# A gMLP layer on one core: the opening transfers regrouped, the first step's twelve products put ahead of the turns, and GpSimd's adding transfers issued in two groups

## The reference

```python
def rms_norm(x, g):
    return x * lax.rsqrt(jnp.mean(x * x, axis=-1, keepdims=True) + EPS) * g

hn = rms_norm(x, norm1_g)
u, v = jnp.split(jax.nn.gelu(hn @ w_in), 2, axis=-1)
v = (v - mu) * lax.rsqrt(var + LN_EPS) * ln_g            # over v's last axis
v = v.reshape(b, l // 128, 128, 8, 256)
ws = jnp.where(causal, w_s, 0)
sv = jnp.einsum('gts,bnsge->bntge', ws, v) + b_s.T[None, None, :, :, None]
x = x + (u * sv.reshape(b, l, 2048)) @ w_out
x = x + jnp.square(jax.nn.relu(rms_norm(x, norm2_g) @ w1)) @ w2
out = rms_norm(x, final_g)
```

## Time and profile before

| | |
|---|---|
| median of 3 runs | 1066.47 us (1065.72 to 1066.68) |
| profiled execution | 1067.01 us |
| span of its instructions | 1064.9 us |
| mean granted TensorE clock | 0.998 |
| PE busy | 1056.5 us (99%) |
| PEld busy | 928.1 us (87%) |
| DVE, ACT, POOL busy | 798.8 us (75%), 561.4 us (53%), 44.5 us (4%) |
| DMA | 206.40 MB, mean 194 GB/s |

### The profile page before, as it was taken

How to read it: one execution, slowest core, us unless ns; L and a number is a source line. 1 busy time by engine, 2 the same in 40 slices (tenths; PEclk the granted TensorE clock), 3 DMA queues, 4 the chain that set the end, 5 groups by cost and what they waited for, 6 DMA issues and landing times.

```text
span 1064.9 us, 13170 instructions
## 1 busy us (share of the span) xinstructions
PE 1056.5 (99%) x5040; PEld 928.1 (87%) x5040; DVE 798.8 (75%) x892; ACT 561.4 (53%) x883; POOL 44.5 (4%) x49
## 2 busy tenths in 40 slices
PE   9999999999999999999999999999999999999997
PEld 8888888889899888888888888888888888888886
DVE  6986666779789996899858457565599585777766
ACT  6864454553554444564874555455643443344456
POOL 0000100000000000111000000000000000000240
PEclk9999999999999999999999999999999999999999
DMA  9273369772876495755444636627878355343224
GB/s 323 73 166 151 112 208 307 180 262 98 320 281 229 156 338 201 200 190 160 151 166 158 198 118 213 208 106 278 323 296 317 135 218 198 119 158 119 82 77 159
DMA packets 89935, 206.40 MB, mean 194 GB/s; under 512 B 9560, under 2 KB 16240, under 8 KB 82672
## 3 DMA queue, kind: packets, MB, share of 16 engines
q1 hardware_dynamic: 86192, 195.32, 52.6%
q0 software_dynamic: 3488, 9.96, 3.9%
q10 hardware_dynamic: 192, 0.27, 0.1%
HBM read 143.67 MB, written 67.11 MB: 198 GB/s over the span
## 4 chain that ended last, share of the span: by engine, by line
PE 98%; DMA 1%; ACT 0%; DVE 0%; SPq 0%; issue 0%; ACTq 0%; DVEq 0%
PE banks L479 32%; PE banks L483 32%; PE banks L484 32%; PE banks L573 3%; DMA rows<-in_x_dram 1%; PE banks L618 0%; ACT rows L1195 0%; PE banks L604 0%; PE banks L529 0%; PE banks L534 0%; DVE rows L1706 0%; ACT spare L1228 0%; ACT rows L1477 0%; DVE ring_low L1536 0%; ACT ring_high L1047 0%
## 5 line engine op out<-in xcount | busy, mean ns | idle before, releaser
L1077 ACT ACTIVATE pair_high<-left_and_right 128x1024 fp32r<-128x1024 f32 x168 | 176.5, 1055 | 223.3 <-PE banks L479 183.9
L1536 DVE TENSOR_TENSOR ring_low<-left_and_right,ring_high 128x512 fp32r<-128x512 f32 x224 | 152.3, 690 | 160.9 <-ACT ring_high L1047 160.3
L1544 DVE TENSOR_TENSOR pair_low<-left_and_right,pair_high 128x1024 fp32r<-128x1024 f32 x168 | 205.1, 1235 | 84.2 <-ACT pair_high L1077 83.9
L479 PE MATMUL banks<-pair_high 128*128 128x512 f32 x672 | 254.9, 379 | 0.0
L483 PE MATMUL banks<-pair_low,pair_high 128*128 128x512 f32 x672 | 254.7, 379 | 0.0
L484 PE MATMUL banks<-pair_high,pair_low 128*128 128x512 f32 x672 | 254.7, 379 | 0.0
L1047 ACT ACTIVATE ring_high<-left_and_right 128x512 fp32r<-128x512 f32 x224 | 136.9, 626 | 206.6 <-PE banks L479 126.0
L479 PE MATMUL banks<-s_high,ring_high 128*128 128x512 f32 x384 | 145.8, 380 | 0.0
L483 PE MATMUL banks<-s_low,ring_high 128*128 128x512 f32 x384 | 145.5, 379 | 0.0
L484 PE MATMUL banks<-s_high,ring_low 128*128 128x512 f32 x384 | 145.5, 379 | 0.0
L484 PEld LDWEIGHTS banks<-pair_high,pair_low 128*128 128x128 f32 x672 | 127.0, 189 | 18.0
(11 more groups left out here) (147 smaller groups left out, 1244.6 us busy)
## 6 DMA issues: line engine op xcount, KB each, us to landing
left_and_right<-sums SPq DMA_DIRECT2D x40, 1024.0 KB, 7.5
sums<-rows SPq DMA_DIRECT2D x34, 1024.0 KB, 5.2
left_and_right<-in_mlp_w_dram SPq DMA_DIRECT2D x34, 1024.0 KB, 7.3
left_and_right<-in_a_w_in_dram SPq DMA_DIRECT2D x19, 1024.0 KB, 7.6
v_blocks<-rows SPq DMA_DIRECT2D x8, 1024.0 KB, 7.2
left_and_right<-in_a_w_out_dram SPq DMA_DIRECT2D x8, 1024.0 KB, 10.5
rows<-in_x_dram SPq DMA_DIRECT2D x7, 1024.0 KB, 8.8
right_sums<-in_mlp_w_dram POOLq DMA_DIRECT2D x6, 1024.0 KB, 11.2
```

Source lines behind the costliest of these rows:

```text
L479: first = nc.tensor.matmul(ps[:, bank, :], stat_high, mov_high, start=start, stop=False, skip_group_check=True)
L1077: nc.scalar.activation(pair_high[pair_entry(d, pos, k)][:, :, :], pair_of(d, pos, k), ACT.Copy)\
L1536: nc.vector.tensor_tensor(ring_low[k][:, :], right_place(n, pos)[:, k, :], ring_high[k][:, :].bitcast(F32), ALU.subtract).then_inc(low_don ...
L1544: nc.vector.tensor_tensor(pair_low[e][:, :, :], pair_of(d, pos, k), pair_high[e][:, :, :].bitcast(F32), ALU.subtract).then_inc(low_done, 1)
```

## The change

The x of a11's k-tiles 1, 2 and 3 comes in one transfer of 768 KB in the third place of SP's queue. b11's k-tiles 1 and 2 follow it singly, each with a semaphore, ahead of a12; its k-tile 3 comes behind a12. b21 is loaded in two halves of 512 KB with a22 between them. `first_unit` issues its twelve products one after another, and `first_turn(1)` follows them, directly ahead of the turns of k-tiles 2 and 3. The fillers behind the gains' turn are one in place of two. On GpSimd the copies and additions of t1 and t3 wait for b22 of single 1 in place of b22 of single 2, and stand ahead of the causal mask; t2 and t4 stay behind it and wait for b22 of single 2.

```diff
@@ first_unit @@
                     if m == 0:
                         mm.then_inc(unit_begun, 1)
-                first_turn(1)
                 pe.wait_ge(combo_low, 1)
 ...
                     nc.tensor.matmul(ps[:, banks[m], :], rows_high[:, c], walked(ring_low[0][:, :]), start=False,
                                      stop=False, skip_group_check=True)
+                first_turn(1)
@@ first_turn @@
-                pe.wait_ge(x_landed[["a11_first", "a11_second", "a11_right", "a11_right"][k]], 16)
+                pe.wait_ge(x_landed["a11_rest" if k else "a11_first"], 16)
@@ tensor block @@
             first_turn(0)
             turn_gains()
-            warm(2)
+            warm(1)
@@ sync block @@
+            def load_k(b, first, end, signal):
+                i = places(0)[b]
+                sp.dma_start(quarter[i][:, first:end, :], weight(0, b)[:, first:end, :]).then_inc(signal, 16)
+
             load_x("a11_first", 0, 0, P)
-            sp.dma_start(quarter[0][:, 0:1, :], weight(0, "b11")[:, 0:1, :]).then_inc(first_landed, 16)
-            load_x("a11_second", 0, P, P)
-            sp.dma_start(quarter[0][:, 1:2, :], weight(0, "b11")[:, 1:2, :]).then_inc(second_landed, 16)
-            load_x("a11_right", 0, 2 * P, 2 * P)
+            load_k("b11", 0, 1, first_landed)
+            load_x("a11_rest", 0, P, 3 * P)
+            load_k("b11", 1, 2, second_landed)
+            load_k("b11", 2, 3, third_landed)
             load_x("a12", 0, NB, NB)
-            load(("b11", 0), quarter[0][:, 2:4, :], weight(0, "b11")[:, 2:4, :], quarter_landed[0], "quarter0")
+            load(("b11", 0), quarter[0][:, 3:4, :], weight(0, "b11")[:, 3:4, :], quarter_landed[0], "quarter0")
             load_x("a21", 4, 0, NB)
-            load_weight(0, "b21")
+            load(("b21", 0), quarter[1][:, 0:2, :], weight(0, "b21")[:, 0:2, :], quarter_landed[1], "quarter1")
             load_x("a22", 4, NB, NB)
+            load_k("b21", 2, 4, b21_rest_landed)
             load_weight(0, "b12")
@@ split_high, on ACT @@
                 elif u == 1:
                     act.wait_ge(second_landed, 16)
+                elif u == 2:
+                    act.wait_ge(third_landed, 16)
+                elif (n, pos) == (0, 1) and k >= 2:
+                    act.wait_ge(b21_rest_landed, 16)
                 else:
                     right_ready(n, pos)
@@ gpsimd block @@
-            pool.wait_ge(ws_turned, 2)
-            nc.gpsimd.affine_select(out=ws_t[:, :, :], in_=ws_t[:, :, :], compare_op=ALU.is_ge, fill=0.0, base=0,
-                                    pattern=[[0, GROUPS], [1, P]], channel_multiplier=-1).then_inc(ws_masked, 1)
-            pool.wait_ge(*landed["b22", 2])
+            pool.wait_ge(*landed["b22", 1])
             nc.gpsimd.dma_start(t_of("t1"), weight(4, "b11")).then_inc(t_made["t1"], 16)
 ...
             nc.gpsimd.dma_start(t_of("t3"), weight(4, "b22"), accum_op=ALU.add).then_inc(t_made["t3"], 16)
+            pool.wait_ge(ws_turned, 2)
+            nc.gpsimd.affine_select(out=ws_t[:, :, :], in_=ws_t[:, :, :], compare_op=ALU.is_ge, fill=0.0, base=0,
+                                    pattern=[[0, GROUPS], [1, P]], channel_multiplier=-1).then_inc(ws_masked, 1)
+            pool.wait_ge(*landed["b22", 2])
             pool.wait_ge(t_made["t1"], 32)
```

More of the change, by code:

```diff
@@ L296, in summed_of @@
             return (2, 4, 6)[d] + h
-        x_landed = {b: sem(f"x_landed_{b}") for b in ("a11_first", "a11_second", "a11_right", "a12", "a21", "a22")}
+        x_landed = {b: sem(f"x_landed_{b}") for b in ("a11_first", "a11_rest", "a12", "a21", "a22")}
         quarter_landed = [sem(f"quarter_landed{i}") for i in range(4)]
@@ L348, in trunk @@
         second_landed = sem("second_landed")
+        third_landed = sem("third_landed")
+        b21_rest_landed = sem("b21_rest_landed")
         x_summed = sem("x_summed")
```

## The result

The changed kernel takes **1067.88 us** (median of 20 runs, 1067.33 to 1068.68). The kernel before takes 1066.41 us in 20 runs beside them (1065.26 to 1066.87). The ratio is 1.0014, with a 95% interval of 1.0008 to 1.0020: about 1.5 us slower, where 1066.3 was forecast. That is less than 0.2%, and just inside the range, but more than the runs leave uncertain. The profiled execution took 1067.86 us (span 1065.5).

A forecast was written before the change was run, and what follows sets the result against it. TensorE, 98% of the chain, bounds the kernel, so only its waits count. Start +1.0 and stall -1.0 sum to 0.0 against the median 1066.47; leaning 0.2 lower gives 1066.3 us, range 1065.3 to 1067.9.

The forecast's parts named there:

- the adding transfers: GpSimd's additions move earlier, so the load of v takes about 4.7 us and TensorE's wait at 227 goes: -1.0 us.
- the stall: TensorE's wait for DVE's `ring_low` at 226.61 to 227.81 us, sized 1.0 us, expected to go entirely.
- The start: First 16 us: unit 2 starts at 16.0 against 15.02, a cost of 1.0 us, between 0.8 and 1.7.
- Late landing: Rival, chance 0.12: the 768 KB land at 9.5 or later; start +1.7, stall -1.0: 1067.2 us.
- The stall stays: Rival, chance 0.11: load of v slow for other traffic, or t4 past 209; start +1.0, stall 0: 1067.5 us.
- The 0.2 us by which the forecast leaned lower: Taken off the sum because the start's terms have slack: the clock may rise earlier, 0.1 us may not be paid.
- One filler less: Ahead of the first products: a filler takes about 0.43 us, so L521 may start at 5.55 instead of 5.99.
- The twelve products: Start: with eight products moved ahead of the turn of k-tile 1, TensorE is free for it at 8.6.
- The 768 KB: Start: the one transfer of x lands at 8.7, bounds 7.3 to 9.5; the turn of k-tile 1 starts at 8.75.
- What is late next: ACT's and DVE's chain behind the turn: 2.76 us, TensorE idle some 1.5, unit 1 at 11.6, unit 2 4.4 later.
- The clock did not fall back: Rival, chance 0.04: the 1.5 us gap before unit 1 drops TensorE to 1.2 GHz, losing 2.6 us: 1068.9 us.
- Nothing new: Added traffic from 86 to 110 us, or b21's later half, might make TensorE wait; the former got no chance of its own.

The follow-up runs named there:

- e1: The kernel before with only the change's GpSimd part (copies and additions of t1 and t3 earlier): 1066.50 us, ratio 1.0001.
- e3: e1 with the turn of k-tile 1 behind the twelve products and one filler, queue of before: 1068.11 us, ratio 1.0013.
- e6: The kernel before with one more wait ahead of GpSimd's chain of copies and additions, which then began at 156.05 against 155.78: 1066.72 us, ratio 1.0004.
- e5: The changed kernel with the 768 KB cut into two transfers again, 256 KB and 512 KB: 1067.22 us, ratio 1.0011.
- e9_after: One more profiled execution of the changed kernel, unedited: 1067.87 us.
- e7: The changed kernel with the second filler put back: 1067.80 us, ratio 1.0017.
- e2: The changed kernel without its GpSimd part: 1068.61 us, ratio 1.0018.
- e4: The changed kernel with the turn of k-tile 1 back between the four and the eight other products, and two fillers: 1067.72 us, ratio 1.0018.
- e9_before_1: One more profiled execution of the kernel before, unedited: 1066.55 us.
- e8: e1 with b11's k-tile 2 in a transfer of its own, with its own semaphore, ahead of a12: 1066.76 us, ratio 1.0002.

## Why the prediction was wrong

**The step that failed** is "All of it goes: -1.0 us" in *the adding transfers*, which the sum then set against the median. In the change the stall is not there, with the times that were reckoned: additions from 87.67, t4's issued at 184.13, a load of v of 4.8 us, `normalise` 1.77 us sooner though the start was later. But the stall belonged to the one execution that was profiled. In three more of before it is missing. There t4's addition is issued at 201.57 to 201.86 rather than 206.08, and lands, 9.4 to 9.6 us later, at 211.0 to 211.4; the load of v is issued at 209.00 to 209.74 and takes 4.9 to 5.3 us. Seen in one execution of four, the term is worth about 0.25 us and not 1.0, an estimate from few executions, and e1 put it at +0.1 us, between -0.9 and +1.0, which just shuts out the -1.0. The warning stood in the prediction: the profiled execution was 0.5 us above the median of the runs. I read that as an offset to subtract at the end; the trace has the same 0.5 us behind the stall (227.81 against a mean of 227.28 in the other three), so the -1.0 was taken from a time that did not hold it.

**The start** was forecast at +1.0 at unit 2, between 0.8 and 1.7, and this term was too small as well. Unit 2 starts at 15.02 in the mean of the four executions of before and at 16.77 in both of the change: +1.75. The step that missed here is the landing of the 768 KB, 9.5 in place of 8.7, which is the whole difference. Further on the difference shrinks by 0.4 us, since in two of the executions of before the turn of a22 stands for x (1.02 us, and about 0.25), and in the change it does not: the product ahead of the stall's place (226.61, 227.24, 226.61 and 227.34; mean 226.95) comes at 228.32 in both executions of the change, +1.37 us. Less the 0.25 this is +1.1, and the program's last product shows the same (1058.8 against a mean of 1057.7). The profiled times of the six executions give 1067.87 - 1066.54 = +1.3; the medians give +1.47 with an interval of 0.9 to 2.1. So two rivals held in part. "Late landing" describes the start, and against the one profiled execution of before also the sum (+0.7; measured 1067.86 - 1067.01 = +0.85). "The stall stays" has the right worth for the additions at the median, though not the cause: nothing stayed, there was mostly nothing to remove. The 0.2 us by which the forecast leaned lower did not come either.

*One filler less* was priced at 0.43 us; the start of L523 at 5.55 was wrong for the two executions of the change. Its weights were split by ACT at 5.29 + 0.63 = 5.92 in place of 5.48, and TensorE waited for them. ACT itself waited for their landing, and that varies: the split begins at 4.49 to 4.85 in the executions of before, but at 5.29 and 5.05 in e3 and e6, which have the same queue. In e5, where it began at 4.62, L523 did start at 5.57. In e9_after it started at 5.76, and most of the first four products ran at the lower level (1.72 us). e7, with the filler back, has the same median, so it costs and gives nothing that can be measured.

*The twelve products* left TensorE free at 8.66, as reckoned (8.6). *The 768 KB* were taken as 8.7, by bytes between two rows; they landed at 9.5 in both executions of the change, the bound of "late landing", and at 8.6 to 9.3 with the same transfer in e2, e4 and e7 (7.0, 7.4 and 6.8 us after an issue near 1.8). The estimate from the page "DMA: Bandwidth & Descriptors" of the Trainium skill (Anatomy of one DMA), by its 2.0 us and 436 GB/s, was 5.6; no run here had it before 8.6.

*What is late next* held in each term: 2.77 us from the turn to the split's end, a gap of 1.38 us (forecast 1.5), 4.33 us from unit 1 to unit 2 (forecast 4.4). Only the 0.2 us that b11's k-tile 2 was to win is, like the stall, not in every execution of before: from unit 1 to unit 2 it is 4.61 us in the first, 4.67 in e6, and 4.34 to 4.38 in the three others.

*The new order* loses even with x in time. e7 against e6 shows it: +1.86 us at unit 1 and, since e6 then stands at the turn of a22 for x and at 227, +0.4 behind the stall. e5, where x landed near 7.0 while TensorE was busy until 9.99, still has 1.0011. e3's runs show it as well, at 1.0013 (1.4 us) without the large transfer. And e4's show that the large transfer loses without the order, at 1.0018. The two do not add up (e2, with both, has 1.0018, and the change 1.0014), since each alone delays the same chain behind the turn of k-tile 1.

**The clock did not fall back** in the gap: unit 1's products stand 0.22 us apart at once. **Nothing new** waits between 86 and 110 us or in units 4 to 8.

What stays open is the exact share of executions with the stall, which four do not give (with e2 and e6, whose additions begin as in before, it is two of six). Open too is why the chain of additions ran late in the first execution: t4's was issued 4.2 to 4.5 us later than in the other three, and most of that arose behind the issue of t2's addition (187.34, against 186.42 to 187.00). And nothing here shows what sets the moment at which the clock rises.

## What to carry over

A wait that one profile shows is a term of the sum only as often as it occurs. Where the profiled execution lies above the median of the runs, ask first which of its waits the others lack; a second or third profile of the unchanged kernel is the cheapest experiment there is. At the start of a kernel, put the piece that opens the longest chain of other engines (here the turn of k-tile 1) first, and keep TensorE's other work behind it as cover; a transfer should end where its first reader needs it, not where the last does.

## What the runs showed of the hardware

TensorE's change from its lower to its upper level at the start comes at different moments in executions of one and the same program. In the four executions of before, the first four products took 1.25 us, 1.28, 1.93 and 2.05. An earlier rise is not all gain: the executions that start unit 2 earliest wait later, for x of a22 at 22.65 (e9_before_1) and 22.93 (e8), or at 227 (e6).

A 1 MB load took 4.8 to 5.3 us where it lay together with the addition for 2.3 us or less, 8.1 with 3.2 us of overlap (e6), and 8.3 with the whole of it. What makes it long is not shown by this alone: in e6 the addition had landed at 203.02 + 8.9 = 211.9, and the load went on until 208.67 + 8.1 = 216.8.
